# One opening stage for load, norm and bias tables, banded bias stores cut into pieces on the weight queue, and row maxima reduced already negated

## What is computed

```python
h = rms_norm(x, attn_pre_norm[j])
h = dilated_attention_mixer(h, attn_w_in[j], attn_w_out[j], rel_bias)
...
bias = rel_bias[t5_bucket(jnp.maximum(back, 0) * dilation)]
logits = jnp.einsum('bnqrhe,bnkrhe->bnrhqk', qs, kw) * scale + bias
lse = jax.nn.logsumexp(logits, axis=-1)
p = jnp.exp(logits - lse[..., None])
```

## Time and profile before

| | us |
|---|---|
| median of three runs | 4773.1 |
| the profiled execution | 4780.6 |
| its span | 4778.8 |
| TensorE busy in it | 3922.5 (82%) |
| GpSimd busy | 1904.8 (40%) |
| VectorE busy | 2188.2 (46%) |
| first projection starts | 107.97 |

### The profile page before, as it was taken

How to read it: one execution, slowest core, us unless ns; L and a number is a source line. 1 busy time by engine, 2 the same in 40 slices (tenths; PEclk the granted TensorE clock), 3 DMA queues, 4 the chain that set the end, 5 groups by cost and what they waited for, 6 DMA issues and landing times. The chain is left out here.

```text
span 4778.8 us, 50851 instructions
## 1 busy us (share of the span) xinstructions
PE 3922.5 (82%) x18060; PEld 3157.2 (66%) x18060; DVE 2188.2 (46%) x3019; ACT 916.0 (19%) x2199; POOL 1904.8 (40%) x687
## 2 busy tenths in 40 slices
PE   2999997572868858998876689978889988868997
PEld 1777773462756746886765568866668866746886
DVE  1232336485344645453436455534454525645453
ACT  0233332110022221111113111104410112211110
POOL 1434440330033314564454346642145643324663
PEclk9999995785588968999987789988789999968998
DMA  8322220136222212222220022221122222202221
GB/s 130 93 75 80 70 77 14 53 128 121 84 76 72 71 36 80 97 97 75 84 79 0 27 80 96 97 76 53 40 84 97 90 81 81 80 27 80 97 97 66
DMA packets 104714, 362.84 MB, mean 76 GB/s; under 512 B 24614, under 2 KB 51494, under 8 KB 68984
## 3 DMA queue, kind: packets, MB, share of 16 engines
q1 hardware_dynamic: 72000, 319.39, 19.7%
q10 hardware_dynamic: 32568, 41.44, 4.0%
HBM read 334.65 MB, written 30.34 MB: 76 GB/s over the span
## 5 line engine op out<-in xcount | busy, mean ns | idle before, releaser
L292 POOL CAST wh<-raw 128x2048 fp32r<-128x2048 f32 x268 | 509.3, 1900 | 2455.7 <-PE bank L324 2455.7
L294 POOL TENSOR_TENSOR wl<-raw,wh 128x2048 fp32r<-128x2048 f32 x268 | 1257.7, 4693 | 21.5
L322 PE MATMUL bank<-XTh,wh 128*128 128x512 f32 x2320 | 930.5, 401 | 70.4 <-DVE XTl L2572 40.8
L323 PE MATMUL bank<-XTh,wl 128*128 128x512 f32 x2320 | 916.9, 395 | 0.0
L324 PE MATMUL bank<-XTl,wh 128*128 128x512 f32 x2320 | 916.0, 395 | 0.0
L322 PEld LDWEIGHTS bank<-XTh,wh 128*128 128x128 f32 x2320 | 444.5, 192 | 188.2 <-issue 89.7
L324 PEld LDWEIGHTS bank<-XTl,wh 128*128 128x128 f32 x2320 | 443.5, 191 | 95.0
L323 PEld LDWEIGHTS bank<-XTh,wl 128*128 128x128 f32 x2320 | 444.7, 192 | 90.1
L322 PE MATMUL bank<-wh,XTh 128*128 128x512 f32 (+2 forms) x1056 | 395.5, 375 | 54.5 <-PEq L463 26.0
L322 PE MATMUL bank<-wh,HTh 128*128 128x512 f32 x1024 | 404.5, 395 | 0.0
L323 PE MATMUL bank<-wh,HTl 128*128 128x512 f32 x1024 | 404.5, 395 | 0.0
(11 more groups left out here) (314 smaller groups left out, 5052.1 us busy)
## 6 DMA issues: line engine op xcount, KB each, us to landing
raw<-in_weights SPq DMA_DIRECT2D x270, 1024.0 KB, 4.8
MO<-ssm_out SPq DMA_DIRECT2D x8, 1024.0 KB, 4.8
B<-bias_d ACTq DMA_DIRECT2D x8, 1024.0 KB, 5.6
bias_d<-tb ACTq DMA_DIRECT2D x1, 4096.0 KB, 63.5
B<-bias_a ACTq DMA_DIRECT2D x8, 512.0 KB, 3.6
ssm_out<-CA SPq DMA_DIRECT2D x16, 256.0 KB, 2.7
ssm_in<-W2T SPq DMA_DIRECT2D x8, 512.0 KB, 2.8
ssm_out<-lag_kernel SPq DMA_DIRECT2D x16, 256.0 KB, 5.2
```

What stands on the lines that cost most here:

```text
L292: pool.tensor_copy(wh[s][:, :], raw[r][:, :]).then_inc(w_high.h, 1)
L294: pool.tensor_tensor(wl[s][:, :], raw[r][:, :], wh[s][:, :].bitcast(F32), ALU.subtract).then_inc(w_split.h, 1)
L322: nc.tensor.matmul(psum, sh, mh, start=first, stop=False)
L323: nc.tensor.matmul(psum, sl, mh, start=False, stop=False)
```

## The change

Three things are changed.

1. `setup` and `norm_phase("pre")` become one block, `begin`. `X` is loaded first, in four pieces on SyncE's queue, ahead of chunks 0 and 1. ScalarE squares a piece as soon as it is there; the norm's gain is multiplied in by VectorE with the row factor, from a copy of the gain on all partitions, and no longer after the transposition. The table matmuls come behind the transpositions. GpSimd splits chunk 0 after the row factors, and chunk 1 in the block of the dilated attention. The copies of the tables out of PSUM are VectorE's first work there.
2. The banded stores move from ScalarE's queue to SyncE's, into the block of the dilated attention, between the weight loads: with every third load from chunk 2 to 23 the three DMAs of `bias_a` for two heads (512 KB in all), with each load from chunk 24 to 39 `bias_d` and `bias_s` of one head (384 KB). ScalarE waits for its piece before each load of `B`; its passes are written out instead of looped.
3. The row maxima are written negated by `tensor_reduce` itself, in all three kinds of attention; the sink is taken in by a minimum with the negated sink, which is made once per run, and the log-sum-exp subtracts instead of adding. Beside that GpSimd's copy of the high part becomes a `tensor_scalar` by 1.0.

```diff
-            pool.tensor_copy(wh[s][:, :], raw[r][:, :]).then_inc(w_high.h, 1)
+            pool.tensor_scalar(wh[s][:, :], raw[r][:, :], 1.0, None, ALU.mult).then_inc(w_high.h, 1)
...
+                        for tt in range(TT):
+                            sp.dma_start(X[:, tt, :], xt[:, tt, :]).then_inc(x_in[tt].h, 16)
+                        for k in range(2):
                             sp.dma_start(raw[k][:, :], t["weights"][k]).then_inc(raw_in[k].h, 16)
...
+                        for tt in range(TT):
+                            rsqrt(tt)
+                        split_high(pool, 0)
+                        split_low(pool, 0)
...
+                        for n in range(2 * TT):
+                            tt, half = n // 2, n % 2
+                            pe.wait_ge(scaled.h, tt + 1)
+                            if n >= 4:
+                                pe.wait_ge(low.h, n - 3)
...
+                        pe.wait_ge(oh_in.h, 16 * 4)
...
+                            v.scalar_tensor_tensor(N[:, tt, :], X[:, tt, :], st[:, tt:tt + 1], gain[:, :], ALU.mult, ALU.mult).then_inc(scaled.h, 1)
+                        for tt in range(TT):
+                            halves(tt)
...
-                            sp_stream(sp, 40)
-                            wait_bias_stored(sp)
+                            for n in range(SPLIT, SPLIT + 40 + RAW):
+                                load_chunk(sp, n, n % RAW)
+                                if n == SPLIT:
+                                    sp.wait_ge(tables.h, 4)
+                                if n < 24 and n % 3 == 2:
+                                    k = n // 3
+                                    heads = slice(2 * k, 2 * k + 2)
+                                    toeplitz(sp, bias_a[heads, :, 0:W1], tab[heads], 0, W1, bias_a_stored[k])
+                                    toeplitz(sp, bias_a[heads, :, W1:384], tab[heads], L1, W2, bias_a_stored[k])
+                                    toeplitz(sp, bias_a[heads, :, 384:512], tab[heads], L1 + L2, W2, bias_a_stored[k])
+                                if 24 <= n < 40:
+                                    h, row = slice(n - 24, n - 23), slice(32 + n - 24, 33 + n - 24)
+                                    toeplitz(sp, bias_d[h], tab[row], 0, WD, bias_ds_stored)
+                                    toeplitz(sp, bias_s[h], tab[row], LD_, WS, bias_ds_stored)
...
+                                act.wait_ge(bias_a_stored[k].h, 16 * 3)
+                                act.dma_start(B[:, :, :], bias_a[2 * k:2 * k + 2].rearrange("h p w -> p h w")).then_inc(BIAS_IN.h, 16)
...
-                        link(v.tensor_reduce(self.stat(n, 0)[:, k:k + m], bands(SC[:, n % DEPTH, :], c, m, w), AX.X, ALU.max))
+                        r = v.tensor_reduce(self.stat(n, 1)[:, k:k + m], bands(SC[:, n % DEPTH, :], c, m, w), AX.X, ALU.max, negate=True)
...
-                    v.tensor_scalar(self.stat(n, 1), self.stat(n, 0), -1.0, None, ALU.mult).then_inc(BIASED.h, 1)
+                        r = v.tensor_scalar(self.stat(n, 1), self.stat(n, 1), self.sink(x)[1], None, ALU.min)
+                    r.then_inc(BIASED.h, 1)
...
-                                    link(v.tensor_reduce(sa[:, n % 2, 0:2], SC[:, n % 2, :, 0:w], AX.X, ALU.max))
+                                    v.tensor_reduce(sa[:, n % 2, 2:4], SC[:, n % 2, :, 0:w], AX.X, ALU.max, negate=True).then_inc(BIASED.h, 1)
```

More of the change, by code:

```diff
@@ L372, in setup @@
                 rb = sb("rb", [33, 2 * HEADS], F32, c)
-                made = signal("made")
-                tables = signal("tables")
+                N = sb("N", [P, TT, D], F32, c)
+                gain = sb("gain", [P, D], F32, c)
+                made, oh_in = signal("made"), signal("onehots_in")
+                x_in = [signal(f"x_in{tt}") for tt in range(TT)]
+                squared, scaled, turned, gain_in = signal("squared"), signal("scaled"), signal("turned"), signal("gain_in")
+                high, low = signal("x_high"), signal("x_low")
+                HOLD = (0, 1, 6, 7)
+                xt = t["x"].rearrange("b (t p) d -> p (b t) d", p=P)
                 with nc.Block() as block:
@@ L435, in _, with halves, toeplitz @@
                     def _(dve):
-                        for n, (o, lo, hi) in enumerate(((ta, 0, 512), (ta, 512, LA), (tb, 0, 512), (tb, 512, LB))):
-                            dve.wait_ge(p_b.h, n + 1)
-                            nc.vector.tensor_copy(o[:, lo:hi], PS[n][0:HEADS, 0:hi - lo]).then_inc(tables.h, 1)
-                loaded.base += 16 * 9
-                p_b.base += 4
+                        v = nc.vector
+                        link = InOrder(dve, dve_order)
+                        def halves(tt):
+                            for n in (2 * tt, 2 * tt + 1):
+                                half = n % 2
+                                dve.wait_ge(high.h, n + 1)
+                                xs = (slice(None), slice(4 * half, 4 * half + 4), slice(P * tt, P * tt + P))
+                                v.tensor_tensor(XTl[xs], PS[HOLD[n % 4]][:, :].rearrange("p (k c) -> p k c", k=4), XTh[xs].bitcast(F32),
+                                                ALU.subtract).then_inc(low.h, 1)
+                        dve.wait_ge(gain_in.h, 16)
+                        for tt in range(TT):
+                            dve.wait_ge(g_b.h, g_b.base + tt + 1)
+                            v.scalar_tensor_tensor(N[:, tt, :], X[:, tt, :], st[:, tt:tt + 1], gain[:, :], ALU.mult, ALU.mult).then_inc(scaled.h, 1)
+                        for tt in range(TT):
+                            halves(tt)
+                        dve.wait_ge(loaded.h, 16 * 3)
+                        link.done()
+                loaded.base += 16 * 3
+                g_b.base += TT
+        def toeplitz(eng, dst, table, off, w, sig):
+            x = table[:, off:off + w]
+            src = bass.AP(x.tensor, x.offset + P - 1, [list(x.ap[0]), [-1, P], [1, w]])
+            eng.dma_start(dst, src).then_inc(sig.h, 16)
         BN = [st[:, 16 + 12 * tt:28 + 12 * tt] for tt in range(TT)]
@@ L1206, in dve_links @@
             def dve_links(self):
-                return sum(len(x.bias) - 1 + len(x.rows) + (self.sink is not None) + 1 + len(x.rows) - 1 for x in self.jobs)
+                return sum(len(x.bias) - 1 + len(x.rows) - (self.sink is None) + 1 + len(x.rows) - 1 for x in self.jobs)
             def act(self, at, copy_to, link=None, drain=lambda j: None):
@@ L1433, in _ @@
                                     place_v(act, 0, 0, 0, V_TILE.index(n - 1))
-                            with act.Fori(0, PASSES - 1) as i:
-                                one_pass(i, False)
-                            one_pass(PASSES - 1, True)
+                            for i in range(PASSES):
+                                one_pass(i, i == PASSES - 1)
                         @block.vector
@@ L2588, in build @@
         with ExitStack() as b_scope:
-            with ExitStack() as a_scope:
-                setup(a_scope, b_scope)
-                if "attn" in STAGES:
-                    norm_phase("pre", gain=col[:, 0:KT], before_end=wait_bias_a_stored)
-                else:
-                    norm_phase("plain", before_end=wait_bias_stored)
-            if "attn" in STAGES:
-                dilated_attention()
+            tab = sb("tab", [32 + HEADS, LB], F32, b_scope)
+            begin(tab)
+            dilated_attention(tab)
         if "attn" in STAGES:
```

121 lines of the change are left out of this document (66 added, 55 removed).

## The result

The changed kernel takes 4838.2 us (median of 4 runs, 4832.9 to 4843.8) where the kernel before takes 4773.6 beside it: a ratio of 1.0132, with a 95% interval of 1.0102 to 1.0162. It is 65 us slower. The forecast was 4705, and its slower case, 4897, rested on another mechanism. The profiled execution has a span of 4837.0 us. The opening did what was forecast; the loss lies behind it, in nearly every stage.

What follows compares the result with a forecast made beforehand. TensorE, busy 82% of the span, was taken as the bound, its largest wait the opening. 4780.6 - 82.5 (opening) + 31 (stores) - 17 (maxima) = 4712.1 us profiled; 7.5 less gives 4705 for the median, range 4660 to 4755.

Steps and rivals of the forecast that it cites:

- its slower case, 4897: Rival, chance 0.13: stores reading one partition starve TensorE of weights in chunks 24 to 39, costing 223 us at 28 us a piece.
- Part 1, the opening: Kernel start: the first projection starts at 25.5 us instead of 107.97, a gain of 82.5 us (73 to 86).
- Part 2, the stores: Banded stores between weight loads on SyncE's queue: they make late weight loads cost 31 us.
- the step that sized the piece: Stores out of one partition: a 384 KB piece takes 16 us, between bounds of 4.0 and 64 us.
- rival 1: Banded stores: they stay hidden, a 384 KB piece taking under 14 us; 4674 us in all; chance 0.27.
- The 31 us at chunks 31 to 39: GpSimd's split and TensorE wait there for late weight loads: 59 us of queue delay less 28 us slack.
- the slack of 28: Weight queue: it may fall behind by 28 us in all before TensorE feels it.
- the lower bound: Stores: a 384 KB piece out of one partition takes 4.0 us if the 99 GB/s of 16 partitions hold.
- Part 3, the maxima: Attention layers: row maxima written negated, without a separate negation, gain 17 us (bounds 8 to 30).
- GpSimd's `tensor_scalar`: High part of each chunk's split: taken to last as long as the copy's 1.90 us, so no change.
- -5 to +11 us: GpSimd's split: the effect put on its new instruction, counting only at stage starts and in ties with VectorE.
- up to 2.8 us more per chunk are covered: GpSimd's split: its waits for TensorE, 9.2 us each before 268 copies, hide up to 2.8 us more per chunk.

Runs made afterwards that it cites:

- e3_copy_oldmax: e1_copy with the row maxima of the kernel before (reduction, then a separate negation): 4697.1 us, ratio 0.9824.
- e11_twice: The changed kernel with tensor_copy, each piece of bias_d and bias_s written a second time to tensors that nothing reads: 4868.0 us, ratio 1.0185.
- e4_before_max: The kernel before with the negated row maxima alone: 4751.3 us, ratio 0.9937.
- e1_copy: The changed kernel with GpSimd's high part as a tensor_copy again, all else as changed: 4671.6 us, ratio 0.978.
- the delay run: The changed kernel with tensor_copy and 118 one-column memsets between copy and subtraction of each split: 4749.8 us, ratio 0.9942.

## Why the prediction was wrong

**Part 1, the opening: right.** Forecast 82.5 us, measured 107.97 - 26.14 = 81.8; with the copy it is 84.0, to 23.93. The gain is carried on: at the output projection of the dilated attention e3_copy_oldmax is 82.0 us ahead of the kernel before (744.95 against 826.96), and 82 at the end.

**Part 2, the stores: the step that sized the piece failed, and rival 1 was right.** The piece was put at 16 us by a slope between 128 and 16 partitions carried on to one; it takes 12.3 to 13.3. The 31 us at chunks 31 to 39 did not come. e11_twice bears the model of the queue out, where it is the bound: by that working a doubled piece at 12.5 us would cost 175 us, measured 196, and with the measured period the slack of 28 us gives 16 x (29.5 - 15.4) - 28 = 198. That 4.0 us, the lower bound, was not the answer, and the upper one neither, shows why both had to be kept.

**Part 3, the maxima: right mechanism, term too small.** 17 us were forecast, 25.5 and 27.5 measured beside the fast copy, within the bounds of 8 to 30. Dilated attention gave what was forecast (8.1 us between the profiled executions of e4_before_max and the kernel before, forecast 7.7); the differential layers gave 10.7 and 5.2, where 9.6 were put for both. That the sum is above by 10 us can't be laid to one wait, with stages that differ by 6 us between two executions of one kernel. Beside the slow form it is 67. The negating reduction costs what the plain one does, as taken.

**GpSimd's `tensor_scalar`: the step that failed and decided the result.** Its working was: "Its bounds are below the copy's 1.90 us and the 4.69 us of the two-input step; one input and the same tile make the copy the nearest: no change." The upper bound was no bound. The form takes 5.45 us, more than the step with two inputs. Likeness in inputs and tile said nothing of its speed, since the same name with one more operation runs at 1.9. By that the term "-5 to +11 us" was in truth 167.

The second half of that step failed as well: "up to 2.8 us more per chunk are covered", and beyond it "-5 to +11 us". Even at the right price, 3.5 us more, it would have charged little. GpSimd's wait for TensorE before each chunk is real (9.2 us before, 6.2 after), and between stages' ends it does cover the split, for TensorE waits for the low part 6.6 us in all. What it does not cover is the split that stands last in a stage or pass or first in a sliding run, 22 times 3.5 us, and VectorE, which is slowed beside GpSimd and in the mixers has no such slack. The prediction itself had read VectorE's long negations as GpSimd's work, and then priced a longer GpSimd step by GpSimd's own waits.

By the parts, against e1_copy: -82 for opening and stores, -25.5 for the maxima, +167 for the slow form, +59 in all; the direct comparison gives +65. Each number holds for the order in which the parts are taken here. Without the slow form the forecast of 4705 would have been 33 us too high, and rival 1's 4674 right to 3 us. That is closer than its working was: rival 1 says 99 us less than before, and e1_copy is 107 below the kernel before that ran beside it (4778.9), the 8 us being those of part 3.

What stays open: why the form with one operation is slow, which no run here can show; how the 88 us beyond lateness divide between waits behind a slowed VectorE and the 40 us that TensorE is busy longer, and what brings the latter; how lateness alone makes TensorE wait longer in differential attention; and whether the hold of the subtraction costs anything, since cutting it gains nothing while cutting the `tensor_scalar` gains 112 us.

## What to carry to other kernels

An instruction that stands in no row of the trace has no upper bound in a row of another kind: measure it alone, with its exact operands, before it goes into a loop of 268. When GpSimd's time per step grows, its slack against TensorE is only one of three ledgers; count also the last step of each stage, which the block's end waits for, and VectorE's instructions of the kinds that were held here (two inputs in SBUF, or a `tensor_scalar` of a few numbers). A store may leave a partition at 30 GB/s and still be free, if one weight load and one piece fit into a chunk period: work out that sum, and double the piece once to see how near the edge it is.

## What the runs showed of the hardware

- GpSimd, 128x2048: `tensor_scalar` with one operation 5.37 us, with two 1.90, `tensor_copy` 1.90, `tensor_tensor` 4.50 (VectorE idle). 128x512: 1.49 with one operation, 0.61 for the copy.
- Beside any of them VectorE's reduction (one input in SBUF) and its addition with one input in PSUM keep 0.69 us; a `tensor_scalar` of 2 numbers, 0.17 us alone, lasts until GpSimd's instruction ends, up to 5.21 (one beside each of nine).
- A VectorE `tensor_tensor` of 128x512 with two inputs in SBUF, 0.69 us alone, ends 0.55 us after a GpSimd `tensor_tensor` that it meets (64 of 64 in e1_copy, 4.31 to 4.33 us), but more than 1.1 us before a one-operation `tensor_scalar` (at most 3.86).
- 118 memsets of one column in a row on GpSimd take 3.41 us, 0.029 each, though each is shown with 0.098: they overlap.
- Stores of 256 and 128 KB out of one partition leave at 30 to 32 GB/s together (worked out from a period of 29.5 us); from 16 partitions the 256 KB land 5.4 us after their issue instead of 14.0.
- TensorE, busy with the same work, is busy 40 us longer in the kernel in which it waits 136 us more, at a mean granted clock of 0.865 instead of 0.876; in the delay run it waits 80 us more and is busy 1 us longer, at 0.872.
